# Products of the identity with itself taken out of TensorE's waits for norms

## The reference

```python
def rmsnorm(x, g):
    xf = x.astype(jnp.float32)
    y = xf * lax.rsqrt(jnp.mean(xf * xf, axis=-1, keepdims=True) + EPS)
    return (y * g.astype(jnp.float32)).astype(x.dtype)
...
    for l in range(DEPTH):                       # first block
        h = rmsnorm(x, mix_norm[l])
        p = jnp.einsum('bsd,dn->bsn', h, w_in[l])
        ...
        x = x + jnp.einsum('bsn,nd->bsd', mix, w_o[l])
        h = rmsnorm(x, ffn_norm[l])
        g = jnp.einsum('bsd,df->bsf', h, w_gate[l])
        u = jnp.einsum('bsd,df->bsf', h, w_up[l])
        x = x + jnp.einsum('bsf,fd->bsd', jax.nn.silu(g) * u, w_down[l])
...
        # second block, for 512 latent tokens and, in its first layer, 256 context tokens
        x = x + g1 * rmsnorm_2(y_lat, norm_g[l, 1])
        x = x + g2 * rmsnorm_2(swiglu(modulate(x, norm_g[l, 2], sh2, sc2), ffn_w_in[l], ffn_w_out[l]),
                             norm_g[l, 3])
```

## Time and profile before

| | us |
|---|---|
| median of three runs | 3062.62 |
| lowest, highest | 3060.34, 3067.62 |
| the profiled execution, its own time | 3063.84 |
| its span, first to last instruction | 3061.9 |
| TensorE busy (matmuls) | 2984.9, 97% |
| VectorE, ScalarE, GpSimd busy | 1706.8, 1178.8, 1236.8 |
| mean granted TensorE clock | 0.990 |

### The profile page before, as it was taken

How to read it: one execution, slowest core, us unless ns; L and a number is a source line. 1 busy time by engine, 2 the same in 40 slices (tenths; PEclk the granted TensorE clock), 3 DMA queues, 4 the chain that set the end, 5 groups by cost and what they waited for, 6 DMA issues and landing times.

```text
span 3061.9 us, 41128 instructions
## 1 busy us (share of the span) xinstructions
PE 2984.9 (97%) x16292; PEld 2488.1 (81%) x16292; DVE 1706.8 (56%) x2810; ACT 1178.8 (38%) x1826; POOL 1236.8 (40%) x584
## 2 busy tenths in 40 slices
PE   8999999999999999999999999999999999999999
PEld 7768888786688888888888998878878789788887
DVE  4656677846563553654528866576594468431113
ACT  4553222246455333234337555532123435432222
POOL 4223444432276333333444554354445220244442
PEclk9999999999999999999999999999999999999999
DMA  8214554522244223224333333355653210123331
GB/s 134 66 56 128 167 174 150 172 59 70 76 138 141 86 70 93 81 67 131 111 90 97 115 114 107 121 158 176 189 165 110 70 63 1 42 74 103 101 98 68
DMA packets 480432, 323.86 MB, mean 106 GB/s; under 512 B 102520, under 2 KB 447744, under 8 KB 479728
## 3 DMA queue, kind: packets, MB, share of 16 engines
q1 hardware_dynamic: 475472, 309.60, 34.6%
q10 hardware_dynamic: 2656, 6.30, 0.6%
q0 software_dynamic: 2112, 5.32, 0.6%
HBM read 315.90 MB, written 5.24 MB: 105 GB/s over the span
## 4 chain that ended last, share of the span: by engine, by line
PE 89%; DVE 7%; ACT 2%; issue 1%; POOL 1%; DMA 0%; DVEq 0%; ACTq 0%; POOLq 0%
PE G L2981 13%; PE G L2990 13%; PE G L2991 12%; PE G L2995 12%; PE G L3221 5%; PE G L3222 5%; PE G L3226 5%; PE G L3008 3%; PE G L4143 1%; PE SS L3350 1%; PE G L3456 1%; PE MM L3350 1%; PE G L3442 1%; DVE acc L1773 1%; PE G L3387 1%
## 5 line engine op out<-in xcount | busy, mean ns | idle before, releaser
L771 POOL TENSOR_TENSOR WL<-raw,WH 128x1024 fp32r<-128x1024 f32 (+1 forms) x520 | 1193.8, 2318 | 1715.9 <-ACT WH L842 1715.9
L842 ACT ACTIVATE WH<-raw 128x1024 fp32r<-128x1024 f32 (+1 forms) x520 | 493.5, 996 | 579.9 <-PE G L3226 379.1
L2990 PE MATMUL G<-hH,WH 128*128 128x512 f32 x1520 | 595.2, 392 | 0.7 <-ACT xtok L1577 0.7
L2991 PE MATMUL G<-hL,WH 128*128 128x512 f32 x1520 | 591.8, 389 | 0.0
L2995 PE MATMUL G<-hH,WL 128*128 128x512 f32 x1520 | 359.9, 389 | 0.0
L2990 PEld LDWEIGHTS G<-hH,WH 128*128 128x128 f32 x1520 | 285.4, 188 | 64.6 <-issue 3.3
L2995 PEld LDWEIGHTS G<-hH,WL 128*128 128x128 f32 x1520 | 285.3, 188 | 59.2
L2991 PEld LDWEIGHTS G<-hL,WH 128*128 128x128 f32 x1520 | 285.4, 188 | 58.4
L1773 DVE SCALAR_TENSOR_TENSOR acc<-adaw,cvec,acc 128x512 f32<-128x512 f32 x280 | 283.9, 1067 | 4.2
L1801 DVE TENSOR_TENSOR FH<-silu,G 128x512 fp32r<-128x512 f32 x44 | 30.3, 688 | 235.1 <-PE G L2995 180.8
L2981 PE MATMUL G<-hH,WH 128*128 128x512 f32 (+1 forms) x416 | 160.4, 386 | 0.0
(11 more groups left out here) (827 smaller groups left out, 5976.3 us busy)
## 6 DMA issues: line engine op xcount, KB each, us to landing
raw<-ffn_w_in_in SPq DMA_DIRECT2D x264, 256.0 KB, 3.4
adaw<-ada_w_in SPq DMA_DIRECT2D x48, 1024.0 KB, 5.2
raw<-ab_w_in_in SPq DMA_DIRECT2D x128, 256.0 KB, 3.0
raw<-ffn_w_out_in SPq DMA_DIRECT2D x96, 256.0 KB, 2.9
raw<-w_gate_in SPq DMA_DIRECT2D x88, 256.0 KB, 3.3
raw<-w_up_in SPq DMA_DIRECT2D x88, 256.0 KB, 3.4
raw<-w_down_in SPq DMA_DIRECT2D x64, 256.0 KB, 3.0
raw<-w_in_in SPq DMA_DIRECT2D x40, 256.0 KB, 3.5
```

Of the source, the lines that this page charges most:

```text
L771: nc.gpsimd.tensor_tensor(low(c)[:, cut], raw[c % 2][:, cut], high(c)[:, cut].bitcast(F32), ALU.subtract)\
L842: nc.scalar.activation(high(c)[:, cut], raw[c % 2][:, cut], ACT.Copy).then_inc(weights_hi, 1)
L2990: mm(dst, view(high(c), k), xh, start=(k == 0 and not (joint and i)), stop=False)
L2991: mm(dst, view(high(c), k), xl, start=False, stop=False)
```

## The change

The set `AWAKE` becomes empty, so `keep_busy` issues nothing. Its calls, and every wait, stay. 114 products go: 18 each at b0.n1, b0.n2 and b1.n1, 12 at t.y1 with t.n2, 36 at t.y2 with m.n1, 12 at m.y1 with m.n2.

```diff
--- before.py
+++ after.py
@@ -3032,7 +3032,7 @@
 
             stats_before = [None]
 
-            AWAKE = {"b0.n1", "b0.n2", "b1.n1", "t.y1", "t.n2", "t.y2", "m.n1", "m.y1", "m.n2", "m.y2"}
+            AWAKE = set()
 
             def keep_busy(n, times):
 
```

## The result

The changed kernel takes 3071.77 us, median of nine runs (3070.37 to 3073.99), where the kernel before takes 3065.28, median of nine (3060.34 to 3070.69): 1.0026 of the time before, with a 95% interval from 1.0017 to 1.0034. It is slower, by little, and by more than its measurement is uncertain. The two medians differ by 6.5 us, or 0.21%; the ratio is estimated over all the executions and stands at 0.26%. The two profiled executions differ by more: 3073.99 against 3063.84.

What follows compares the result with a forecast made beforehand. TensorE, busy for 97% of the span, was taken to bound the kernel. From the profiled 3063.84 us, 7.5 less for delayed work and 13.0 more for the lower clock gave 3069.3 us; range 3063 to 3075.

Steps and rivals of the forecast that it cites:

- That products delay ready work: At b0.n1, b0.n2, b1.n1, t.y2, t.n2 and m.n2, ready work stands behind products; removing them saves 7.5 us.
- The lower clock in the openings: At b0.n1, b0.n2, b1.n1 and m.n1, 4.4 us of each opening run low: 8.2 us more.
- Rival B: Long fall: 5.6 us low in each of four openings, all spreads low; +10.8 us, 3074.6 us; chance 0.13.
- Spreads and sums: Half of the spreads at b0.n2, b1.n1, t.y2, m.n1 run low, +1.9 us; sums at the first three, +0.6.
- m.n2: The second spread starts 2.3 us earlier, low clock costs 0.95 there and 0.2 in the opening: -1.15 us.
- The slack of the openings: VectorE paces the openings at t.n2 and m.n2, so a low clock costs only 0.2 us each.
- A: Short fall: 3.2 us low in each of four openings, spreads mostly over before; +1.6 us, 3065.4 us; chance 0.20.
- C: The clock doesn't fall, or only where it costs nothing; only the 7.5 us saving remains, 3056.3 us; chance 0.05.
- D: Transposes of x ahead of b0.n1's opening don't hold the clock; 2.8 us more, 3072.1 us at most; chance 0.07.

Runs made afterwards that it cites:

- first_off: Kernel before without its products at b0.n1, b0.n2 and b1.n1 alone; ratio 1.0007 to the kernel before.
- transposes_twice: Kernel before with each product of the identity replaced by two transposes of the identity; ratio 1.0005.
- double: Kernel before with twice as many products everywhere; ratio 1.0073.
- openings_only: Kernel before without the products ahead of the sums and the spreads, and between the two spreads of t.n2 and m.n2; ratio 0.9996.
- sums_only: Kernel before without the products ahead of the spreads and the openings; ratio 1.0009.
- trimmed: Kernel before with b0.n1's eight moved before the weights' wait, six ahead of b1.n1's sums, three at t.y2, four between spreads at t.n2 and m.n2; ratio 0.9991.
- filled2: trimmed plus twelve products each ahead of the openings of t.n2 and m.n2 and before t.n1's wait for weights; 3057.75 us, 0.9984 of the kernel before.
- second_off: Kernel before without its products at t.y1, t.n2, t.y2, m.n1, m.y1 and m.n2 alone; ratio 1.0019.
- transposes: Kernel before with each product of the identity replaced by one transpose of the identity; ratio 1.0009.
- one_col: Kernel before with each product cut to one column instead of 128; ratio 1.0085.

## Why the prediction was right, point by point

The forecast was 3069.3 us, +6.7 over the median then known and +0.22%; measured were 3071.77, +6.5 us (0.21% by the medians, 0.26% by the ratio) against a kernel before whose median over nine runs is 3065.28. The direction, the size and the mechanism held. Not every term did, and the sum came out in part by luck, as the last but one point tells.

**That products delay ready work: right at the places, too high for b0.n2.** At t.y2 the sums now start 0.15 us behind VectorE's added squares, with 1.47 us of idle time ahead of them, where they had stood 1.4 us behind the earlier trace rows:

```profile
2398.70 1.03 PE L3061 MATMUL MM<-ones,rstd 128*128 128x1 f32 x8 [1.47 <-DVE rstd L1708]
...
2397.87 0.68 DVE L1708 TENSOR_TENSOR rstd<-rstd,sq 128x512 f32<-128x512 f32 x1
```

2397.87 + 0.68 = 2398.55, so the step from VectorE to TensorE takes 0.15 us, which the prediction had left out: each gain ahead of the sums was too large by about 0.1 us. They measured 0.15, 0.40 and 1.26 us at b0.n2, b1.n1 and t.y2, forecast 0.25, 0.5 and 1.35. At b0.n1 the opening stands 1.8 us earlier, where 1.3 were forecast. The doubled products confirm the term from the other side.

**The lower clock in the openings: the right mechanism, mis-sized.** The prediction took 4.4 us low in each of four. Measured in the profile after: 5.0, 4.4, 6.0 and 5.6, mean 5.25. By its own factor that makes 21.0 x 0.468 = 9.8 us and not 8.2; the openings' lengths grew by 2.37, 1.94, 2.63 and 2.13, 9.1 us. The two rows from which 4.4 came, 3.2 and 5.6, follow waits in which other work or a shorter idle time stood. Rival B had 5.6 us low in each of the four, and the low time came out nearer to B's than to the forecast's.

**Spreads and sums: twice the forecast.** The prediction let half of the spreads run low. In this execution all four do: 2.08 us at b0.n2, 2.01 at b1.n1, 2.08 at t.y2 and 2.07 at m.n1, against 1.16 in each before; that is 3.6 us and not 1.9. From the first sum to the spread b0.n2, b1.n1 and t.y2 need 1.4 us more in all, and not 0.6. Earlier starts of 3.6 us and costs of 9.1 + 3.6 + 1.4 = 14.1 make the +10.45 of the table's b0.n1, b0.n2, b1.n1 and t.y2 with m.n1.

**m.n2: the step that failed.** The prediction had -2.3 + 0.95 + 0.2 = -1.15 us and the profiles have +1.84. It let the sums of y1 run as before, and gave the four products ahead of them no worth. TensorE at m.y1 before, and after:

```profile
2666.29 1.05 PE L3959 MATMUL MM<-ones,sq 128*128 128x1 f32 x8 [0.46 <-ACT sq L888]
...
2668.99 1.14 PE L3116 MATMUL MM<-ident,ncol 128*128 128x128 f32 x8
```

```profile
2675.14 1.86 PE L3959 MATMUL MM<-ones,sq 128*128 128x1 f32 x8 [1.35 <-ACT sq L888]
2676.86 3.55 PE L3959 MATMUL SS<-ones,m_five 128*128 128x1 f32 x16
2680.28 2.05 PE L3116 MATMUL MM<-ident,ncol 128*128 128x128 f32 x8
2683.26 2.08 PE L3116 MATMUL SS<-ident,ncol 128*128 128x128 f32 x8 [0.93 <-DVE ncol L2467]
2688.90 0.77 PE L3008 MATMUL G<-hH,WH 128*128 128x512 f32 x1 [3.57 <-DVE hL L2449]
```

The clock fell at 2672.7, ahead of them; the 24 records took 5.14 us, from 2675.14 to 2680.28, where they had taken 2.70. The second spread does follow the reciprocal directly, but from the first spread to the second that saves 1.4 us and not 2.3, since the first now runs low too (2.05 us for 1.14). At t.n2 the same 24 records had run low in the profile of before too, so there the saving stayed, and -0.65 was forecast and -0.79 measured.

That the products ahead of these sums matter can be read over all the profiles. In the eight kernels with at least eight records of 128 columns there (before, first_off, transposes_twice, double, openings_only, sums_only, trimmed, filled2) the 24 records took 2.6 to 2.9 us at 12 of the 16 places, and 5.1 at four: t.y1 in before and filled2, m.y1 in trimmed and filled2. In the four others (after, second_off, transposes, one_col) they took 4.7 to 5.1 us at all eight. An estimate from these counts: 0.75 x 2.4 = 1.8 us on average at each of t.y1 and m.y1, which the prediction has at nothing.

**The slack of the openings: there at t.n2, not at m.n2.** At t.n2 2.9 us ran at the lower level, and the opening takes 14.55 us from its first matmul to the next product's first, before and after. The prediction read the idle time in the earlier trace rows, of t.n2, and gave m.n2 the same slack. But there four transposes of x stand behind each six matmuls (L3087), and hardly any idle time is left: in filled2, all at the upper level,

```profile
2677.45 0.40 PE L3008 MATMUL G<-hH,WL 128*128 128x512 f32 x1
2677.68 0.60 PE L3087 MATMUL G<-ident,xT 128*128 128x128 f32 x4
2678.38 0.47 PE L3008 MATMUL G<-hH,WH 128*128 128x512 f32 x1
```

m.n2's opening took 17.15 us with nothing low (filled2), 18.12 with 4.2 us low (after) and 18.79 with 5.6 (before). So it pays for the low clock. In the difference this stayed hidden, since it ran low before too.

**Why the sum still came out.** The places of the two profiles sum to +11.5 us, twice the forecast's 5.5, the median shows +6.5. The profiled execution of before lies 1.4 us below the median of its kernel, that of after 2.2 above (3073.99, the highest of nine): these make the 3.7 us between 10.15 and 6.5. And places of chance are large beside that: first_off, whose program at t.y1 and t.n2 is that of before, has -1.94 us there, so the profile of before was a slow one at that place, while b0.n1 in second_off, again unchanged, is 2.26 us slower than in it. Which places make up the rest of an average can't be read, since only one execution of each kernel has a trace. The openings (8.2 of 9.1 us), the spreads (1.9 of 3.6) and the sums (0.6 of 1.4) were under-priced and m.n2 missed by 3 us, and the median still fits: that is in part luck.

**The rivals.** A (a short fall, 3065.4) and C (no fall) are out by the stretches after. B (a long fall, +10.8) describes the profiled execution better than the forecast does: all four spreads low, 5.25 us low in the openings where it has 5.6, sums at 1.4 where it has 1.3, and +10.15 in all. The median of 3071.77 lies between the two, 2.5 us above the forecast and 2.8 below B. D said that transposes don't hold the clock: in the profile after TensorE has nothing but the transposes of x ahead of 14.57 us, and the stretch from 10.3 is at 1.00:

```profile
7.29 5.33 PE L3468 MATMUL G<-ident,xin 128*128 128x128 f32 x32 [7.29 <-DMA ident<-tables_in]
14.57 1.16 PE L3116 MATMUL MM<-ident,ncol 128*128 128x128 f32 x8 [1.96 <-DVE ncol L1840]
...
10.30:17.00 6.70, 3.47 (x28) 1.00 1.13 289
```

The clock's own records begin only at 10.2 us, so the starts have to tell the level ahead of that: the transposes start every 0.21 us up to 10.1 and every 0.11 from 10.3 on. So transposes raise the clock as well as hold it, and D is out.

## What to carry to other kernels

Where TensorE bounds a kernel, look at the granted clock around each of its waits, and price a wait without work at the lower level's share in the opening behind it: here 4.4 to 6.0 us at half the clock, which cost 1.9 to 2.6 us, behind 7 to 12 us without a large product. Add the small products inside the wait, each spread 0.9 us longer. Work that is there only to hold the clock pays off in idle time and costs its full length in front of ready work, so it belongs in the idle time alone, and no more of it than fits. Here products of 128 columns did it, and transposes that took as long; products of one column didn't. A single profile of such a kernel places its cost, but its total is another matter: some ten runs of each kernel gave it to about 3 us to each side here, since low stretches come and go with nothing changed.

## What the runs showed of the hardware that I had not expected

A transpose of a 128 x 128 float32 tile takes half of the time of the product with the identity (sixteen took 1.91 us, sixteen products 3.73), and it raises and holds the clock. One-column products don't, though TensorE's busy time reads the same: it was recorded busy for 2.90 of 2.90 us before the clock fell. At the lower level they take nearly twice as long too, 3.41 us for sixteen records instead of 1.84, and so do their weight loads, 0.213 us from one to the next instead of 0.112. And the clock fell, with an unchanged program, at 19.3 us in one execution and not in another, worth 1.6 us there. Over the executions of one kernel, 0.004 of mean clock goes with some 7 us of time (0.987 against 0.991).
